# An eight-column product behind the first three products of four weight pieces

## The reference

```
# first block, memory cross-attention (m = 256 memory tokens)
k, v = jnp.split(mem @ w_xkv, 2, axis=-1)
sc = jnp.einsum('bshd,bmhd->bhsm', q, k) * XA_HEAD_DIM ** -0.5
o = jnp.einsum('bhsm,bmhd->bshd', softmax(sc), v)
h = h + o.reshape(b, s, 1024) @ w_xo
# then: mixture of 32 experts (about 96 MB of weights)
...
# second block, feed-forward part, D_FF = 2816
gate, up = jnp.split(u @ w_gate_up[i], [D_FF], axis=-1)
y = (jax.nn.silu(gate) * up) @ w_down[i]
```

## Time and profile before

| what | us |
|---|---|
| median of 3 runs | 1059.7 (1051.88, 1061.1, 1059.7) |
| the profiled execution's own time | 1060.42 |
| its span, from first to last instruction | 1058.6 |
| TensorE products busy | 997.8 (94%) |
| weight loads busy | 921.5 (87%) |
| DVE busy | 626.3 (59%) |
| ACT busy | 514.3 (49%) |
| mean granted TensorE clock | 0.982 |

### The profile page before, as it was taken

How to read it: one execution, slowest core, us unless ns; L and a number is a source line. 1 busy time by engine, 2 the same in 40 slices (tenths; PEclk the granted TensorE clock), 3 DMA queues, 4 the chain that set the end, 5 groups by cost and what they waited for, 6 DMA issues and landing times.

```text
span 1058.6 us, 19412 instructions
## 1 busy us (share of the span) xinstructions
PE 997.8 (94%) x8564; PEld 921.5 (87%) x8564; DVE 626.3 (59%) x831; ACT 514.3 (49%) x693; POOL 19.7 (2%) x23
## 2 busy tenths in 40 slices
PE   7999999999999999998987677699999999999998
PEld 6999999899989999996664444499999999999998
DVE  6798789867767865542110110279985755555566
ACT  5576497844675563532110111277667653443453
POOL 0000021001000000000000000000000000000000
PEclk9999999999999999999998988999999999999999
DMA  7665453446145456699999999675423265545531
GB/s 286 240 239 191 168 199 127 180 155 223 74 174 185 160 205 233 254 415 380 421 421 421 420 420 422 271 284 167 152 80 114 108 228 199 197 171 195 194 121 41
DMA packets 34871, 241.74 MB, mean 228 GB/s; under 512 B 4064, under 2 KB 4448, under 8 KB 6368
## 3 DMA queue, kind: packets, MB, share of 16 engines
q1 hardware_dynamic: 33264, 233.32, 58.1%
q0 software_dynamic: 1232, 6.99, 1.8%
q10 hardware_dynamic: 288, 0.15, 0.1%
HBM read 239.36 MB, written 1.08 MB: 227 GB/s over the span
## 4 chain that ended last, share of the span: by engine, by line
PE 77%; DMA 12%; DVE 7%; ACT 2%; issue 1%; SPq 1%; DVEq 0%
PE ps L473 18%; PE ps L475 18%; PE ps L474 18%; DMA wr<-in_c_weights 5%; DMA raw<-in_c_weights 4%; PE ps L562 3%; PE ps L1250 3%; DMA xlo<-in_c_weights 3%; PE ps L1216 2%; DVE wlo L2001 2%; PE ps L951 1%; PE ps L1290 1%; PE ps L1277 1%; DVE xs L2227 1%; ACT whi L1349 1%
## 5 line engine op out<-in xcount | busy, mean ns | idle before, releaser
L2001 DVE TENSOR_TENSOR wlo<-raw,whi 128x2048 fp32r<-128x2048 f32 (+1 forms) x119 | 271.1, 2281 | 114.6 <-ACT whi L1349 114.2
L473 PE MATMUL ps<-XUh,whi 128*128 128x256 f32 x992 | 280.6, 283 | 0.3 <-DVE XUl L2007 0.3
L474 PE MATMUL ps<-XUl,whi 128*128 128x256 f32 x992 | 276.6, 279 | 0.0
L475 PE MATMUL ps<-XUh,wlo 128*128 128x256 f32 x992 | 276.6, 279 | 0.0
L1349 ACT ACTIVATE whi<-raw 128x2048 fp32r<-128x2048 f32 (+1 forms) x119 | 225.0, 1893 | 48.7 <-PE ps L475 40.0
L473 PEld LDWEIGHTS ps<-XUh,whi 128*128 128x128 f32 x992 | 186.6, 188 | 2.6 <-issue 2.3
L474 PEld LDWEIGHTS ps<-XUl,whi 128*128 128x128 f32 x992 | 188.0, 190 | 0.7 <-issue 0.5
L475 PEld LDWEIGHTS ps<-XUh,wlo 128*128 128x128 f32 x992 | 186.5, 188 | 0.0
L1250 PE MATMUL ps<-wr,Xg 128*32 128x256 f32 x480 | 56.3, 456 | 22.5 <-DMA wr<-in_c_weights 10.0
L2926 DVE SCALAR_TENSOR_TENSOR sphs<-sphs,wsl,ps 128x256 f32<-128x256 f32 x8 | 3.8, 481 | 95.1 <-ACT sphs L1966 95.1
L1250 PEld LDWEIGHTS ps<-wr,Xg 128*32 128x32 f32 x480 | 28.4, 131 | 35.8 <-issue 31.8
(11 more groups left out here) (617 smaller groups left out, 2352.6 us busy)
## 6 DMA issues: line engine op xcount, KB each, us to landing
raw<-in_c_weights SPq DMA_DIRECT2D x139, 1024.0 KB, 4.9
wr<-in_c_weights SPq DMA_DIRECT2D x36, 1024.0 KB, 26.6
xhi<-in_c_weights SPq DMA_DIRECT2D x12, 1024.0 KB, 26.8
xlo<-in_c_weights SPq DMA_DIRECT2D x12, 1024.0 KB, 27.2
extra<-in_c_weights SPq DMA_DIRECT2D x10, 1024.0 KB, 27.7
acb<-sums POOLq DMA_DIRECT2D x4, 1024.0 KB, 5.0
T<-in_c_weights SPq DMA_DIRECT2D x4, 1024.0 KB, 25.8
T8b<-in_c_weights SPq DMA_DIRECT2D x4, 1024.0 KB, 27.0
```

The source lines that it names most:

```text
L473: pe.matmul(ps, h(k), xh(k), start=start and k == 0, stop=False, skip_group_check=loose)
L474: pe.matmul(ps, h(k), xl(k), start=False, stop=False, skip_group_check=loose)
L475: t = pe.matmul(ps, l(k), xh(k), start=False, stop=stop and k == kt - 1, skip_group_check=loose)
L2001: dve.tensor_tensor(l[:, 0:n], r, h[:, 0:n].bitcast(F32), ALU.subtract).then_inc(*did("w_lo", "split", i))
```

## The change

`triple` gets a parameter `short`, a place in the accumulator. Where it is given, one more product is issued behind the three products of k = 0: the weights of k = 1 by the first 8 of the 256 moving columns. It goes to the first 8 columns of the second half of the same bank. The second half is begun later with `start=True`, so what the short product wrote there is overwritten. Four pieces get one such product each, in their first half: cross values piece 0, cross output piece 0, feed-forward gate 1 and up 1. No wait, semaphore, load or buffer is changed.

```diff
-        def triple(ps, h, l, xh, xl, kt, ready=None, start=True, stop=True, loose=False):
+        def triple(ps, h, l, xh, xl, kt, ready=None, start=True, stop=True, loose=False, short=None):
             for k in range(kt):
+                if short is not None and k == 1:
+                    pe.matmul(short, h(k), xh(k)[:, 0:8], start=False, stop=False, skip_group_check=True)
                 if ready is not None:
                     w.wait_ge(*ready(k))
...
# chunk
-                           lambda k: xh[:, k, :], lambda k: xl[:, k, :], kt, ready)
+                           lambda k: xh[:, k, :], lambda k: xl[:, k, :], kt, ready, short=ps[:, 256:264] if name == "xo" and c == j == 0 else None)
...
# chunk_tok
-                           lambda k: h[:, k, :], lambda k: l[:, k, :], kt, ready)
+                           lambda k: h[:, k, :], lambda k: l[:, k, :], kt, ready, short=ps[:, 256:264] if name == "xv" and c == j == 0 else None)
...
# ffn_up
-                           lambda k: XUh[:, k, :], lambda k: XUl[:, k, :], 8, ready)
+                           lambda k: XUh[:, k, :], lambda k: XUl[:, k, :], 8, ready, short=ps[:, 256:264] if j == 0 and c == 1 else None)
```

## The result

The changed kernel's median is 1060.33 us (22 launches, 1057.96 to 1064.98); before has 1057.93 us in 22 launches beside it (1051.22 to 1062.05). The ratio is 1.0037, 95% interval 1.002 to 1.0055: slower by 0.4%, where 0.6% faster was forecast. The profiled execution of the changed kernel took 1061.41 us, with a span of 1059.6.

The account below looks back on a forecast made before the run. TensorE's own pace was taken to bound the feed-forward part, weight loads the experts' stage. From the profiled 1060.4, less 6.5 (feed-forward) and 0.5 (values), output 0: 1053.4, stated as 1053.2 us; range 1049.5 to 1061.

Parts of the forecast that it names:

- the condition under feed-forward: Feed-forward stream: 1509 products turn fast at gate 1 and stay so past up 1; -6.7 + 0.22 = -6.5 us.
- half a redraw: Rival: feed-forward turns fast, then slow at the second short product, values go fast; 1059.9 us, chance 0.09.
- 0.5 us for values turned fast: Cross values: 141 products at the fast pace, -0.63 + 0.11 = -0.5 us, counted in full.
- a new draw with good odds: Slow product streams: an interruption redraws the pace, kept until the next one; the nearest small case went fast.
- two interruptions read: Profile rows: at 713.95 us slow became fast without idle; at 199.78, behind 1.18 us idle, fast went mostly to slow.
- The two paces of 113.3 and 117.8 ns: Product streams of the same form at full clock: two paces, 4.4 ns apart, kept until something interrupts.
- The price of a short product: Each added 8-column product on TensorE: 0.11 us, set by its weight load; bounds 0.11 and 0.20.
- no redraw: Rival: short products leave all streams slow and only add their price; 1060.8 us, chance 0.14.
- values and output count for little: Cross values counted -0.5 us; cross output counted 0, bounds -0.7 and +0.1, given back waiting for weights.
- the burst of expert loads: Behind cross values: the burst starts at 437.77 us and should start 0.5 us earlier if the values end earlier.

Follow-up runs that it names:

- e1: Before plus only the short product of feed-forward gate 1; ratio to before 1.0034 (1.0008 to 1.0059), 3 of 12 launches below 1057 us.
- e4: Before plus an 8-column short product in every split piece that goes through the three functions (96 in all); 1074.18 us, 19.6 above before.
- e12: The kernel of e9 again, on the chip of e11; median 1054.99 us, ratio to before 0.9961 (0.9934 to 0.9988).
- e3: Before plus only the short products of cross values and cross output, none in feed-forward; ratio to before 0.9989 (0.9968 to 1.0009).
- e11: The changed kernel itself, unaltered, measured again beside e12 and before on one chip; median 1059.59 us, ratio to before 1.0018 (0.9986 to 1.0049).
- e9: Before plus three extra feed-forward products, 128, 8 and 128 columns, in gate 1, up 1, gate 2, without the change's short products; ratio to before 1.0007 (0.9986 to 1.0029).

## Why the prediction was wrong

**The step that failed** is the condition under feed-forward, in its second half: "6.7 us if the stream goes fast there and the second one, 48 products later, leaves it so". The stream did go fast at the first short product, and the second took it back. That is the rival called half a redraw, to which I gave 0.09; its 1059.9 compares with 1061.41 for the profiled execution (it had also counted 0.5 us for values turned fast, which stayed slow). Behind it lies a wrong reading of the state: I took an interruption for a new draw with good odds. In the traces it is a fixed map: from fast it leads to slow every time (10 of 10), and from slow to fast from one place of three (12 of 12, against 0 of 29 from the other two).

**What I took for the state of before was one of two.** The profiled launch and two of three shown were slow, and I reckoned against that. Of 22 launches 9 were fast. For a fast start the first short product makes the stream slow (e1), and the second finds it with the long load 3 ahead and leaves it slow (table, and e4's trace from 861 us on); for a slow start the pair gives fast, then slow. Both ends are slow. That is the loss: 9 of 22 launches x (1058.91 - 1052.15) = 2.8 us in the mean, of the 4.2 us between the means of the two (1056.6 and 1060.8).

**The clue was in the rows.** Of two interruptions read, went from slow to fast and the earlier trace rows from fast to slow. I put the second aside as a full stop and let one case stand for the change's. And the earlier trace rows gave only the product's 276 and 281 ns; the weight loads' 188 and 192, in the same view, would have shown that slow has a place in the rhythm of three.

**Right as forecast.** The two paces of 113.3 and 117.8 ns, and that a stream keeps its own until interrupted: every trace from e1 to e12. The price of a short product, 0.11 us. That nearly the whole of the 4.4 ns a product counts in the feed-forward part, 6.7 us by the forecast: from the stream's first product (848.59 us in before, 846.38 in e3) to the end of the span before took 210.0 us with a slow stream and e3 204.0 with a fast one, 6.0 less. The rival no redraw is out, since the first short product did shift the state. The Trainium skill's page "TensorE: Matmul & The Clock Gate", section "Back-to-back issue gap", gives streams of weight load and product one distance for a width, about 81 ns at 128 columns and 131 ns at 512. For 256 columns every trace here has two, 113.3 and 117.8 ns. That values and output count for little: e3's 0.9989 has 1 in its interval. But my -0.5 us for the values never came to a test, since that stream stayed slow. What it leaned on, that the burst of expert loads follows the end of the values, does show: in the ten traces the burst starts 0.23 to 0.25 us behind the start of the last value product, at 438.39 us in the changed kernel.

**Open.** The launches above 1057 are 1.4 us later in the changed kernel (1060.33 against 1058.91), of which two uncovered short products make 0.22 and those in values 0.11. e11 has its median 1.6 us below that of before's 17 launches above 1057 (1061.16), so a scatter of this size comes from elsewhere. In the traces most of it comes from ahead of the feed-forward stream: that starts between 845.8 and 849.6 us in the ten traces, 849.56 in the changed kernel and 848.59 in before. What sets it was not tried. The same scatter may be why the three products look dearer than foreseen: their launches are 2.1 us (e9, 1053.67 against 1051.61) and 3.2 us (e12, 1054.99 against 1051.78) above the median of before's launches below 1057, where 0.4 to 0.7 were expected, although from the start of the stream to the end e9 and e12 took 204.8 and 204.0 us, 0 to 0.8 more than e3. That is argued and not shown. Nor was it tried what makes a stream start fast or slow, and why one series of before has 24 of 29 launches below 1057 us and another 6 of 23.

## What to carry to other kernels

Where much of a kernel is streams of equal products, read its pace from counts and durations, and read several launches before calling one value the kernel's: here a part of the launches, from a quarter to nine in ten of a series, is 7 us faster for no change at all. An interruption that helped in one trace is no improvement until it is known what it does to a stream that was fast already; put it into every piece of one kernel, and a single trace gives most of the table. To bring all launches to the better pace, the map must send two states to one, which the eight-column product doesn't and a sequence with 128-column products does.

## What was not expected of the hardware

Dense streams of weight load (the weights stationary) and 256-column product at the full clock have, in this kernel, four states that last for up to 1500 products: 113.3 ns a product, or 117.8 ns with one load in three at 192 instead of 187 to 188 ns. What an extra product does to the state is reproducible to the product: 51 of 51 settled cases with 8 columns follow one table, and moving two of e9's three extra products by one product turns 12 of 12 launches below 1057 us into 2 of 8. A product of 8 columns costs 0.11 us, and one of 128 columns in the same place also: it was followed after 0.06 us and the next after 0.17, so 0.23 for both (e9, below), as with 8 columns.

Timeline of TensorE in e9 at its third extra product:

```profile
857.59 0.22 PE L475 MATMUL ps<-XUh,whi 128*128 128x128 f32 x1
857.65 0.34 PE L481 MATMUL ps<-XUh,wlo 128*128 128x256 f32 x1
857.82 0.28 PE L477 MATMUL ps<-XUh,whi 128*128 128x256 f32 x1
```
